# Two transformer blocks in one kernel: openings by tiles, conditioning sums one feed-forward step later

## The chip, the core and the metric

The kernel is one program on one core of a Trainium2 chip. A core has five engines that work side by side and meet only at semaphores: TensorE (PE in the profile; its weight loads are PEld), VectorE (DVE), ScalarE (ACT), GpSimd (POOL) and SyncE (SP), which here only issues transfers. Each engine takes its own instructions strictly in the order in which they are written. SBUF is the memory on the core, PSUM the one that TensorE writes its sums to. The metric is the device time of one execution in microseconds (us), as the median of several.

## What is computed

The reference runs a first block of two layers and then a second block of two layers over 256 tokens of width 1024, in float32.

A layer of the first block is conditioned by a vector `c`: `mod = silu(c) @ ada_w + ada_b`, nine vectors of 1024. It has three sublayers: a SwiGLU feed-forward, a token mixer and another SwiGLU feed-forward (inner width 2816), each as

```
u = h * (1 + scale) + shift
y = (silu(u @ w_gate) * (u @ w_up)) @ w_down        # feed-forward
h = layer_norm(alpha * h + 0.5 * gate * y, g, b)
```

The mixer projects `u` to three branches (a gated convolution, a state-space scan, an attention with compressed keys) and merges them. A layer of the second block is an RMS norm, a projection to attention and mLSTM, an output product, and a feed-forward `relu(u @ w_ff1)**2 @ w_ff2` with inner width 4096.

## The kernel before

Activations are kept transposed: 8 tiles of 128 features by 256 tokens. Weights come from memory as chunks of 128 x 1024 numbers (512 KB) into a ring of nine slots (`stream_weights`, issued by SyncE). A large product is made from three fast ones (`product3`, lines 446 to 453): every float32 operand is split into a high part and a low part (the rest), and the sum high x high + high weight x low activation + low weight x high activation stands for the full product. In the trace line 451 is the first of these, 452 the one with the low activation, 453 the one with the low weight; the tile names `ac_parts`, `h_parts`, `cmp_parts` hold high activations, `u_parts` low ones, `high` the high and `ring_parts` the low weights.

So every chunk needs two preparations before TensorE can take it. ScalarE copies its high part (`high`, line 1054, one of three buffers, so it waits until the chunk three places earlier has been used), then the low part is a subtraction: VectorE makes it for the chunks of the gate and up products (`low`, line 1433), GpSimd for those of the down products (`low_down`, line 1968). Count `lo_g` tells TensorE how many of GpSimd's are ready.

A feed-forward of the first block has 22 slices of the inner width. `step` j of its loop (three passes over six steps, j = 0 to 5; in the trace a step's products are 48 matmuls for the two up chunks of slice f = 1 + j and 24 for the down chunk of the slice before) goes like this.
- TensorE: `up` of the next slice (16 tiles of three products), then `down` of the one before. In step 5 it also multiplies the conditioning sum's 8 tiles with a vector of ones, `column_sums` (line 491), between the two.
- ScalarE: silu of the gate half (line 1084), three high parts with the high part of the hidden slice between them.
- VectorE: `hidden` (line 1501, silu x up), a low part, `hidden_low` (line 1505), in steps 0 to 3 two `add_modulation` each (lines 1379 and 1381: conditioning weights of 128 x 1024 times one number for each partition, added into `eb`), then another low part. In step 5 it fetches the column sums.
- GpSimd: `low_down` for the chunk of the next `down`, then, in steps 0 to 3, two `load_later`: each waits until VectorE has counted the matching addition (`ada.used`) and issues the transfer of the next pass's tile into the same place (line 1944). GpSimd's order is `low_down`, load, load, `low_down`, load, load, and so on; in the third pass of a layer's second feed-forward there are no loads.

A stage opens after a normalization. `enter` on VectorE writes eight tiles of `u`; ScalarE copies each one's high part (count `uhi`), VectorE subtracts to the low part (line 1455, or 2617 in the second block, count `ulo`). `up_first` and its like wait for `ulo` of tile k, then run the three products of that tile for both chunks of the pair. The last feed-forward of the second block opens with one chunk only. There are ten openings: four feed-forwards and two mixers in the first block, two projections and two feed-forwards in the second. While TensorE waits for the norm it multiplies zeros (`products_of_zeros`, 128 x 512, bf16).

In the middle of the mixer two small products (line 727, 60 columns wide) wait for two blocks that GpSimd gathers (line 2015, count `kpe`). There are 16 of these matmuls for block `b = 0` and 16 for `b = 1`, each two records in the trace.

## Time and profile before

| | |
|---|---|
| median of 3 runs | 2673.26 us (2667.3 to 2674.91) |
| the profiled execution | 2667.08 us, span 2665.4 us, mean granted clock of TensorE 0.989 |
| TensorE | 2571.5 us busy, 96% of the span |
| VectorE, ScalarE, GpSimd | 1797.8, 1208.2 and 998.0 us |
| the chain that ended last | 86% of it TensorE, 6% VectorE, 3% GpSimd, 3% ScalarE |

The busy time of an engine is the sum of its instructions; the time that matters is that of the chain, in which each piece is what the next one waited for. The granted clock is the one that the chip gave TensorE: 1.00 is 2.4 GHz, 0.50 is 1.2 GHz. Starts in the rows are counted from the start of the span. In the order of time the stages are: start and first conditioning sums to 43 us; first layer's feed-forward to 247, mixer to 740, second feed-forward to 947; the same for the second layer to 1856; and the second block's two layers from there.

### The profile page before, as it was taken

The page shows a single profiled execution, that of the slowest core. Times are in us where ns is not written, and L with a number is a line of the kernel's source. Part 1 is how long each engine was busy: PE and PEld are TensorE (multiplying, and loading weights), DVE is VectorE, ACT ScalarE, POOL GpSimd, SP SyncE. Part 2 cuts the span into 40 slices and gives each one's busy share as a digit, 9 for nine tenths or more (in the row PEclk, how much of TensorE's full clock was granted, in tenths as well). Part 3 has the DMA queues.
Part 4 walks back from the last instruction along what each step waited for, and adds up shares of the span by engine and source line. Part 5 has one row for each costly group of instructions (what it writes and reads, how often), then busy time and mean ns, then how long its engine had stood idle before and what let it go on. Part 6 is the DMA issues. An engine that isn't in the chain of part 4 may idle for free.

```text
span 2665.4 us, 51124 instructions
## 1 busy us (share of the span) xinstructions
PE 2571.5 (96%) x19552; PEld 2420.5 (91%) x19552; DVE 1797.8 (67%) x2822; ACT 1208.2 (45%) x2019; POOL 998.0 (37%) x588
## 2 busy tenths in 40 slices
PE   3999999999999999999999999999999999999999
PEld 3999999888889989989998878999888999988999
DVE  6775898467686577559984666765853576753676
ACT  2444456245554454444552554444552344652444
POOL 2433986200033233358870000333650244650244
PEclk9999999799999999999999999999999999999999
DMA  8775774233477567767643335775434566433464
GB/s 329 250 271 174 264 228 149 88 102 96 142 252 261 174 229 271 248 216 234 198 130 92 103 96 179 274 243 166 132 115 124 152 186 188 147 122 123 152 188 134
DMA packets 131491, 481.28 MB, mean 181 GB/s; under 512 B 14848, under 2 KB 14848, under 8 KB 130560
## 3 DMA queue, kind: packets, MB, share of 16 engines
q1 hardware_dynamic: 107280, 389.12, 46.1%
q0 software_dynamic: 23040, 83.90, 8.6%
q10 hardware_dynamic: 1008, 6.00, 0.6%
q8 instruction: 113, 1.85, 0.3%
q14 instruction: 50, 0.41, 0.0%
HBM read 475.82 MB, written 3.15 MB: 180 GB/s over the span
## 4 chain that ended last, share of the span: by engine, by line
PE 86%; DVE 6%; POOL 3%; ACT 3%; issue 1%; DVEq 1%; DMA 0%; SPq 0%; ACTq 0%; POOLq 0%
PE ps L451 22%; PE ps L453 21%; PE ps L452 21%; PE ps L693 4%; PE ps L2324 2%; PE ps L543 2%; PE ps L2291 2%; POOL ring_parts L1963 1%; POOL eb L2015 1%; PE ps L491 1%; PE ps L920 1%; DVE ring_parts L1433 1%; DVE eb L1381 1%; PE ps L903 1%; PE ps L793 1%
## 5 line engine op out<-in xcount | busy, mean ns | idle before, releaser
L452 PE MATMUL ps<-u_parts,high 128*128 128x256 f32 x3840 | 1087.9, 283 | 0.0
L452 PEld LDWEIGHTS ps<-u_parts,high 128*128 128x128 f32 x3840 | 737.7, 192 | 0.4
L1054 ACT ACTIVATE high<-ring 128x1024 fp32r<-128x1024 f32 x461 | 485.7, 1056 | 395.2 <-PE ps L453 367.7
L451 PE MATMUL ps<-ac_parts,high 128*128 128x256 f32 x1920 | 550.4, 287 | 18.5 <-DVE u_parts L1455 10.0
L453 PE MATMUL ps<-ac_parts,ring_parts 128*128 128x256 f32 x1920 | 545.5, 284 | 0.0
L1968 POOL TENSOR_TENSOR ring_parts<-ring,high 128x1024 fp32r<-128x1024 f32 x88 | 224.9, 2555 | 473.8 <-ACT high L1054 473.8
L451 PE MATMUL ps<-h_parts,high 128*128 128x256 f32 x1360 | 393.7, 289 | 4.5 <-POOL ring_parts L1963 3.6
L451 PEld LDWEIGHTS ps<-ac_parts,high 128*128 128x128 f32 x1920 | 365.9, 191 | 25.1 <-issue 15.9
L453 PE MATMUL ps<-h_parts,ring_parts 128*128 128x256 f32 x1360 | 386.0, 284 | 0.0
L1963 POOL TENSOR_TENSOR ring_parts<-ring,high 128x1024 fp32r<-128x1024 f32 x138 | 331.3, 2407 | 105.0 <-ACT high L1054 103.7
L453 PEld LDWEIGHTS ps<-ac_parts,ring_parts 128*128 128x128 f32 x1920 | 364.2, 190 | 0.0
L1433 DVE TENSOR_TENSOR ring_parts<-ring,high 128x1024 fp32r<-128x1024 f32 x176 | 217.8, 1239 | 199.0 <-ACT high L1054 188.2
L451 PE MATMUL ps<-pt_parts,high 128*128 128x256 f32 x1216 | 340.8, 280 | 0.8 <-DVE pt_parts L1505 0.8
L452 PE MATMUL ps<-pt_parts,high 128*128 128x256 f32 x1216 | 339.0, 279 | 0.0
L453 PE MATMUL ps<-pt_parts,ring_parts 128*128 128x256 f32 x1216 | 339.0, 279 | 0.0
L2810 POOL TENSOR_TENSOR ring_parts<-ring,high 128x1024 fp32r<-128x1024 f32 x64 | 153.7, 2401 | 366.7 <-ACT high L2384 366.5
L2384 ACT ACTIVATE high<-ring 128x1024 fp32r<-128x1024 f32 x195 | 206.1, 1057 | 178.4 <-PE ps L453 113.8
L451 PEld LDWEIGHTS ps<-h_parts,high 128*128 128x128 f32 x1360 | 262.2, 193 | 13.4 <-issue 5.1
L453 PEld LDWEIGHTS ps<-h_parts,ring_parts 128*128 128x128 f32 x1360 | 262.3, 193 | 0.0
L1944 POOL DMA_DIRECT2D xc<-ada_dram x64 | 34.9, 547 | 554.4 <-DVE u L1446 526.8
L453 PEld LDWEIGHTS ps<-pt_parts,ring_parts 128*128 128x128 f32 x1216 | 230.5, 190 | 0.0
L451 PEld LDWEIGHTS ps<-pt_parts,high 128*128 128x128 f32 x1216 | 228.6, 188 | 1.4 <-DVE pt_parts L1505 1.4
(448 smaller groups left out, 4820.5 us busy)
## 6 DMA issues: line engine op xcount, KB each, us to landing
ring<-stream_dram SPq DMA_DIRECT2D x736, 512.0 KB, 3.7
xc<-ada_dram POOLq DMA_DIRECT2D x84, 512.0 KB, 5.8
z<-ada_dram POOLq DMA_DIRECT2D x36, 512.0 KB, 6.7
qr<-ada_dram POOLq DMA_DIRECT2D x36, 512.0 KB, 6.5
h_aside<-ac ACTq DMA_DIRECT2D x2, 1024.0 KB, 4.4
eb<-ada_dram POOLq DMA_DIRECT2D x4, 512.0 KB, 5.2
h<-h_aside ACTq DMA_DIRECT2D x2, 1024.0 KB, 6.0
conb<-con_dram ACTq DMA_DIRECT2D x1, 1032.0 KB, 7.7
```

The source lines that it names most:

```text
L451: mm(out, hi, xh, start=start, stop=False, **kw)
L452: mm(out, hi, xl, start=False, stop=False, **kw)
L453: return mm(out, lo, xh, start=False, stop=stop, **kw)
L543: last = mm(ps[:, bank, 0:S], ones, src[:, n], start=n == 0, stop=n == ND - 1)
L693: last = mm(out, chunk_tile(m, i, k), src[:, k], start=k == 0, stop=k == 7)
L1054: act(high_of(m, i), chunk_of(m, i), ACT.Copy).then_inc(made, 1)
L1433: tt(low_of(m, i), chunk_of(m, i), high_of(m, i), ALU.subtract).then_inc(sem["lo"], 1)
L1963: nc.gpsimd.tensor_tensor(low_of(m, i), chunk_of(m, i), high_of(m, i), ALU.subtract)\
L1968: nc.gpsimd.tensor_tensor(low_of(m, i), chunk_of(m, i), high_of(m, i), ALU.subtract)\
L2291: last = mm(ps[:, unit(k4), c * S:(c + 1) * S], chunk_tile(m, i, 4 * c + k), (m.att, m.hm)[b][:, k], start=k == 0, stop=k == 3)
L2384: act(high_of(m, i), chunk_of(m, i), ACT.Copy).then_inc(sem["hi"], 1)
L2810: nc.gpsimd.tensor_tensor(low_of(m, i), chunk_of(m, i), high_of(m, i), ALU.subtract)\
```

## The change

Five edits:
1. `pair_by_tiles` replaces the loops of all ten openings. It waits for the high part of tile k (`uhi`), runs the two products that need only that (high x high and low weight x high activation) for both chunks, waits for `ulo` of tile k, and then runs the product with the low activation for both chunks. The chunk counts `done` are raised by the last products, one behind the other.
2. The second block's feed-forward opens with a pair of chunks too, and `down` of slice 0 stands right behind it; the rest keeps its order.
3. `column_sums` in step 5 stands behind `down`.
4. VectorE's conditioning additions stand in steps 1 to 4 in place of 0 to 3. GpSimd's program is not edited.
5. More products of zeros: 14 for 11 and 10 for 8 in the second block's norms, and 8 new ones ahead of the first small product of `kpe`.

```diff
--- before.py
+++ after.py
@@ -453,6 +453,20 @@
     return mm(out, lo, xh, start=False, stop=stop, **kw)
 
 
+def pair_by_tiles(t, mm, m, outs, chunks, xh, xl, high, low):
+
+    for k in range(ND):
+        a, b = k * P, (k + 1) * P
+        high(k)
+        for out, i in zip(outs, chunks):
+            mm(out, high_of(m, i)[:, a:b], xh[:, k], start=k == 0, stop=False, skip_group_check=True)
+            mm(out, low_of(m, i)[:, a:b], xh[:, k], start=False, stop=False, skip_group_check=True)
+        low(k)
+        ends = [mm(out, high_of(m, i)[:, a:b], xl[:, k], start=False, stop=k == ND - 1, skip_group_check=True)
+                for out, i in zip(outs, chunks)]
+    return ends
+
+
 def two(ps, bank, a=0, n=256):
     return ps[:, bank, a:a + 2 * n].rearrange("p (n t) -> p n t", n=2)
 
@@ -569,13 +583,11 @@
             def up_first(i):
 
                 t.wait_ge(sem["lo"], at("lo", 2 * NF * q + 2))
-                for k in range(ND):
-                    t.wait_ge(sem["ulo"], at("ulo", 28 * q + k + 1))
-                    for c in range(2):
-                        last = product3(mm, ps[:, 4 + 2 * c, c * S:(c + 1) * S], m, i + c, k, m.uhi_ffn[:, k], m.ulo[:, k],
-                                        start=k == 0, stop=k == ND - 1, skip_group_check=True)
-                        if k == ND - 1:
-                            last.then_inc(done, 1)
+                ends = pair_by_tiles(t, mm, m, [ps[:, 4 + 2 * c, c * S:(c + 1) * S] for c in range(2)], (i, i + 1),
+                                     m.uhi_ffn, m.ulo, lambda k: t.wait_ge(sem["uhi"], at("uhi", 28 * q + k + 1)),
+                                     lambda k: t.wait_ge(sem["ulo"], at("ulo", 28 * q + k + 1)))
+                ends[0].then_inc(done, 1)
+                ends[1].then_inc(done, 1)
 
             def down(i, f, fk, last=False):
                 t.wait_ge(sem["lo_g"], at("lo_g", q * (NF + FRONT) + fk + 1))
@@ -591,9 +603,9 @@
             with t.Fori(0, 3) as it:
                 for j in range(6):
                     up(cb + 2 + 3 * j, 1 + j, 6 * it + 1 + j)
+                    down(cb + 4 + 3 * j, j, 6 * it + j)
                     if j == 5:
                         column_sums(t, mm, m, ada, ada.summed_group(l, q, it))
-                    down(cb + 4 + 3 * j, j, 6 * it + j)
             for f in range(19, NF):
                 up(cb + 3 * f - 1, f, f)
                 down(cb + 3 * f + 1, f - 1, f - 1)
@@ -615,13 +627,11 @@
                 t.wait_ge(sem["sg"], at("sg", 1))
             if n == 0:
                 low_made(C_GLU + 1)
-                for k in range(ND):
-                    t.wait_ge(sem["ulo"], at("ulo", 8 + k + 1))
-                    for c in range(2):
-                        last = product3(mm, ps[:, unit(3 * c), c * S:(c + 1) * S], m, C_GLU + c, k, m.uhi[:, k], m.ulo[:, k],
-                                        start=k == 0, stop=k == ND - 1, skip_group_check=True)
-                        if k == ND - 1:
-                            last.then_inc(done, 1)
+                ends = pair_by_tiles(t, mm, m, [ps[:, unit(3 * c), c * S:(c + 1) * S] for c in range(2)], (C_GLU, C_GLU + 1),
+                                     m.uhi, m.ulo, lambda k: t.wait_ge(sem["uhi"], at("uhi", 8 + k + 1)),
+                                     lambda k: t.wait_ge(sem["ulo"], at("ulo", 8 + k + 1)))
+                ends[0].then_inc(done, 1)
+                ends[1].then_inc(done, 1)
             else:
                 project(C_GLU + 2 * n, ps[:, unit(j), 0:S]).then_inc(done, 1)
                 project(C_GLU + 2 * n + 1, ps[:, unit(j), S:2 * S]).then_inc(done, 1)
@@ -719,6 +729,9 @@
 
         t.wait_ge(sem["rope"], at("rope", 9))
         for b in range(2):
+            if b == 0:
+                for _ in range(8):
+                    mm(ps[:, unit(j), :], m.zero[:, 0:P], m.zero[:], start=True, stop=True)
             t.wait_ge(sem["kpe"], at("kpe", b + 1))
             for c in range(2):
                 i = C_CK + 2 * b + c
@@ -1516,9 +1529,9 @@
                     hidden(f, fk)
                     low(i + 3, HIGHS * q + 3 * fk + 4)
                     hidden_low(f, fk)
-                    if j < 4:
-                        add_modulation(nc, v, m, ada, ada.group(l, 2 * q, it), ada.summed_group(l, q, it), 2 * j)
-                        add_modulation(nc, v, m, ada, ada.group(l, 2 * q, it), ada.summed_group(l, q, it), 2 * j + 1)
+                    if 1 <= j < 5:
+                        add_modulation(nc, v, m, ada, ada.group(l, 2 * q, it), ada.summed_group(l, q, it), 2 * j - 2)
+                        add_modulation(nc, v, m, ada, ada.group(l, 2 * q, it), ada.summed_group(l, q, it), 2 * j - 1)
                     low(i + 5, HIGHS * q + 3 * fk + 6)
                     if j == 5:
                         keep_columns(nc, v, m, ada, ada.summed_group(l, q, it))
@@ -2072,7 +2085,7 @@
                 t.wait_ge(sem["usq"], at("usq", 8 * k + n + 1))
                 last = mm(ps[:, 0, 0:S], con("mean"), m.sq[:, n], start=n == 0, stop=n == ND - 1)
             last.then_inc(sem["uvar"], 1)
-            products_of_zeros(mm, m, (11, 8)[k])
+            products_of_zeros(mm, m, (14, 10)[k])
 
         rms(0)
         j = 0
@@ -2083,13 +2096,11 @@
             return j + 1
 
         t.wait_ge(sem["lo_g"], at("lo_g", E_Q + 2))
-        for k in range(ND):
-            t.wait_ge(sem["ulo"], at("ulo", k + 1))
-            for c in range(2):
-                last = product3(mm, ps[:, unit(3 * c), c * S:(c + 1) * S], m, E_Q + c, k, m.uhi2[:, k], m.ulo[:, k],
-                                start=k == 0, stop=k == ND - 1, skip_group_check=True)
-                if k == ND - 1:
-                    last.then_inc(done, 1)
+        ends = pair_by_tiles(t, mm, m, [ps[:, unit(3 * c), c * S:(c + 1) * S] for c in range(2)], (E_Q, E_Q + 1),
+                             m.uhi2, m.ulo, lambda k: t.wait_ge(sem["uhi"], at("uhi", k + 1)),
+                             lambda k: t.wait_ge(sem["ulo"], at("ulo", k + 1)))
+        ends[0].then_inc(done, 1)
+        ends[1].then_inc(done, 1)
         j += 1
         project(E_IF, ps[:, unit(j), 0:S]).then_inc(done, 1)
         j += 1
@@ -2349,17 +2360,18 @@
                     x.then_inc(pairs, 1)
             x.then_inc(done, 1)
 
-        t.wait_ge(sem["lo"], at("lo", 1))
-        for k in range(ND):
-            t.wait_ge(sem["ulo"], at("ulo", 8 + k + 1))
-            last = product3(mm, ps[:, 4, 0:S], m, E_FFN, k, m.uhi_ffn[:, k], m.ulo[:, k],
-                            start=k == 0, stop=k == ND - 1)
-        last.then_inc(done, 1)
+        t.wait_ge(sem["lo"], at("lo", 2))
+        ends = pair_by_tiles(t, mm, m, [ps[:, 4 + c, 0:S] for c in range(2)], (E_FFN, E_FFN + 1), m.uhi_ffn, m.ulo,
+                             lambda k: t.wait_ge(sem["uhi"], at("uhi", 8 + k + 1)),
+                             lambda k: t.wait_ge(sem["ulo"], at("ulo", 8 + k + 1)))
+        ends[0].then_inc(done, 1)
+        ends[1].then_inc(done, 1)
+        down(E_FFN + 2, 0, 0)
         with t.Fori(0, 3) as it:
             for q in range(9):
-                up(E_FFN + 1 + 2 * q, 1 + q, 9 * it + 1 + q)
-                down(E_FFN + 2 + 2 * q, q, 9 * it + q)
-        for f in range(28, NF2):
+                up(E_FFN + 3 + 2 * q, 2 + q, 9 * it + 2 + q)
+                down(E_FFN + 4 + 2 * q, 1 + q, 9 * it + 1 + q)
+        for f in range(29, NF2):
             up(E_FFN + 2 * f - 1, f, f)
             down(E_FFN + 2 * f, f - 1, f - 1)
         down(E_FFN + 63, 31, 31, last=True)
```

VectorE at the start of the feed-forward loop before (L1501 is `hidden`, L1433 a low part of weights, L1505 `hidden_low`, L1379 and L1381 the additions; rows without a tile are waits and register instructions):

```order
L1432 REGISTER_ALU
L1433 TENSOR_TENSOR ring_parts<-ring,high 128x1024
L1499 REGISTER_ALU
L1501 TENSOR_TENSOR pt<-ps,pt 128x256
L1432 ISA
L1433 TENSOR_TENSOR ring_parts<-ring,high 128x1024
L1505 TENSOR_TENSOR pt_parts<-pt,pt_parts 128x256
L1381 SCALAR_TENSOR_TENSOR eb<-xc,cvec,eb 128x1024 x2
L1432 REGISTER_ALU
L1433 TENSOR_TENSOR ring_parts<-ring,high 128x1024
```

and from the end of `hidden_low` of step 0 in the changed kernel (13 lines further down: L1514 for L1501, L1446 for L1433, L1518 for L1505, L1392 and L1394 for the additions):

```order
L1518 TENSOR_TENSOR pt_parts<-pt,pt_parts 128x256
L1445 REGISTER_ALU
L1446 TENSOR_TENSOR ring_parts<-ring,high 128x1024
L1512 REGISTER_ALU
L1514 TENSOR_TENSOR pt<-ps,pt 128x256
L1445 ISA
L1446 TENSOR_TENSOR ring_parts<-ring,high 128x1024
L1518 TENSOR_TENSOR pt_parts<-pt,pt_parts 128x256
L1387 ISA
L1391 REGISTER_ALU
L1392 TENSOR_SCALAR eb<-xc,cvec 128x1024
L1394 SCALAR_TENSOR_TENSOR eb<-xc,cvec,eb 128x1024
```

The first two additions stood behind the first `hidden_low`; now a low part, a `hidden`, another low part and the second `hidden_low` are between.

GpSimd in the same loop of the changed kernel (L1981 is `low_down`, L1957 the wait for `ada.used` and the transfer into the conditioning tile):

```order
L1981 TENSOR_TENSOR ring_parts<-ring,high 128x1024
L1961 ISA
L1957 ISA
L1957 DMA xc<-ada_dram 128x1024
L1961 REGISTER_ALU
L1957 ISA
L1957 DMA xc<-ada_dram 128x1024
L1980 ISA
L1981 TENSOR_TENSOR ring_parts<-ring,high 128x1024
```

Nothing moved here: the second `low_down` still stands behind the two loads.

TensorE at the opening of the first feed-forward before:

```order
L451 MATMUL ps<-ac_parts,high 128x256
L452 MATMUL ps<-u_parts,high 128x256
L453 MATMUL ps<-ac_parts,ring_parts 128x256
L451 MATMUL ps<-ac_parts,high 128x256
L452 MATMUL ps<-u_parts,high 128x256
L453 MATMUL ps<-ac_parts,ring_parts 128x256
```

and after (L462, L463 and L465 are the three products in `pair_by_tiles`):

```order
L462 MATMUL ps<-ac_parts,high 128x256
L463 MATMUL ps<-ac_parts,ring_parts 128x256
L462 MATMUL ps<-ac_parts,high 128x256
L463 MATMUL ps<-ac_parts,ring_parts 128x256
L465 MATMUL ps<-u_parts,high 128x256 x2
```

Each tile's six products are the same; the two with `u_parts` are now last, behind a wait of their own.

## Rows read from the trace of the kernel before

**Rows 1.** part 1 of the page: busy time, share of the span, instructions
```profile
PE 2571.5 (96%) x19552; PEld 2420.5 (91%) x19552; DVE 1797.8 (67%) x2822; ACT 1208.2 (45%) x2019; POOL 998.0 (37%) x588
```

**Rows 2.** waits of TensorE: line waited for, us in total, times, longest
```profile
PE ps L451 <- DVE u_parts L1455: 10.0, 4, 5.6
PE ps L451 <- DVE u_parts L2617: 6.1, 4, 1.9
...
PE ps L451 <- DVE ring_parts L1433: 5.2, 4, 1.5
PE ps L727 <- POOL eb L2015: 4.3, 2, 2.2
```

**Rows 3.** timeline of TensorE, one step: start, us, instruction
```profile
881.94 0.29 PE L451 MATMUL ps<-pt_parts,high 128*128 128x256 f32 x1
...
890.49 0.29 PE L451 MATMUL ps<-pt_parts,high 128*128 128x256 f32 x1
```

**Rows 4.** timeline of VectorE, two steps of the same loop
```profile
876.44 0.75 DVE L1379 TENSOR_SCALAR eb<-xc,cvec 128x1024 f32<-128x1024 f32 x1
877.28 1.28 DVE L1381 SCALAR_TENSOR_TENSOR eb<-xc,cvec,eb 128x1024 f32<-128x1024 f32 x1
...
882.56 0.42 DVE L1501 TENSOR_TENSOR pt<-ps,pt 128x256 f32<-128x256 f32 x1 [0.65 <-ACT pt L1084]
883.51 1.23 DVE L1433 TENSOR_TENSOR ring_parts<-ring,high 128x1024 fp32r<-128x1024 f32 x1 [0.52 <-ACT high L1054]
884.65 0.42 DVE L1505 TENSOR_TENSOR pt_parts<-pt,pt_parts 128x256 fp32r<-128x256 f32 x1
884.99 4.63 DVE L1381 SCALAR_TENSOR_TENSOR eb<-xc,cvec,eb 128x1024 f32<-128x1024 f32 x2
```

**Rows 5.** timeline of ScalarE, same step
```profile
887.81 1.06 ACT L1054 ACTIVATE high<-ring 128x1024 fp32r<-128x1024 f32 x1 [1.78 <-PE ps L453]
```

**Rows 6.** timeline of GpSimd: a low part, two issues, a low part
```profile
886.11 2.42 POOL L1968 TENSOR_TENSOR ring_parts<-ring,high 128x1024 fp32r<-128x1024 f32 x1 [5.29 <-ACT high L1054]
...
134.79 0.53 POOL L1944 DMA_DIRECT2D xc<-ada_dram  x1 [1.22 <-DVE eb L1381]
...
268.79 1.09 POOL L1944 DMA_DIRECT2D xc<-ada_dram  x2
269.90 2.40 POOL L1963 TENSOR_TENSOR ring_parts<-ring,high 128x1024 fp32r<-128x1024 f32 x1
```

**Rows 7.** timeline of VectorE in the step of the 134.79 issue
```profile
129.51 4.62 DVE L1381 SCALAR_TENSOR_TENSOR eb<-xc,cvec,eb 128x1024 f32<-128x1024 f32 x2
```

**Rows 8.** timelines of VectorE, ScalarE, TensorE, first layer's second feed-forward opening
```profile
757.41 0.49 DVE L1455 SCALAR_TENSOR_TENSOR u_parts<-u,entry,ac_parts 128x256 fp32r<-128x256 f32 x1 [0.18 <-ACT ac_parts L1065]
757.81 1.22 DVE L1433 TENSOR_TENSOR ring_parts<-ring,high 128x1024 fp32r<-128x1024 f32 x1
...
758.71 1.06 ACT L1054 ACTIVATE high<-ring 128x1024 fp32r<-128x1024 f32 x1 [1.34 <-PE ps L453]
...
759.08 0.39 PE L451 MATMUL ps<-ac_parts,high 128*128 128x256 f32 x1
```

**Rows 9.** timelines of VectorE and TensorE, second block's last opening
```profile
2483.99 0.98 DVE L2617 TENSOR_TENSOR u_parts<-u,ac_parts 128x256 fp32r<-128x256 f32 x2
...
2487.57 0.42 DVE L2776 TENSOR_TENSOR pt_parts<-pt,pt_parts 128x256 fp32r<-128x256 f32 x1 [0.83 <-ACT pt_parts L2564]
...
2485.58 0.28 PE L453 MATMUL ps<-ac_parts,ring_parts 128*128 128x256 f32 x1
...
2488.58 0.28 PE L451 MATMUL ps<-pt_parts,high 128*128 128x256 f32 x1
```

**Rows 10.** windows: busy us of each engine, granted clock (PEclk), DMA
```profile
475.10:478.80 3.70, 3.67 (x33) 3.54 (x31) 3.48 (x7) 2.91 (x7) 3.70 (x8) 1.00 0.47 167
481.80:492.00 10.20, 10.20 (x49) 10.20 (x49) 7.09 (x10) 0.67 (x5) 3.91 (x2) 0.50 0.33 116
1393.30:1403.30 10.00, 9.94 (x46) 9.94 (x47) 7.95 (x11) 0.67 (x5) 4.86 (x3) 0.50 0.46 139
```

## The prediction

> **What bounds the kernel now.** I read the page first: TensorE is busy 2571.5 us of 2665.4 [rows 1], so at most 94 us can be won by filling its gaps, and every other engine has slack on average. Then the waits of TensorE: of those that this change could touch, 10.0 + 6.1 us are waits for low activations at openings, 5.2 us for a low weight part by VectorE, 4.3 us for GpSimd's gathered blocks [rows 2]. The rest of the gaps is mostly the start. Last the timelines of one loop step on each engine. They show that the loop is TensorE's alone: a `down` starts at 881.94, the next at 890.49, 8.55 us later, with no bracketed idle time at either [rows 3]. Call the start of `down` T; all times below are counted from it.
>
> **The additions one step later: what is queued behind them.** On VectorE the move costs nothing by itself. Steps 1 to 4 get what steps 0 to 3 had. And it wins nothing: the low parts that TensorE waits for (5.2 us in 4 waits, one at each feed-forward [rows 2]) are made ahead of step 0's additions, so they come as late as before.
>
> But the additions release GpSimd. Its order is unchanged: `low_down`, load, load, `low_down`. The two loads behind the `low_down` of step j wait for two additions that now run in step j + 1, and the `low_down` of step j + 1, which TensorE needs for its next `down`, is queued behind them. Before, it started at T + 4.17 (886.11) and ended at T + 6.59, 1.96 us ahead of the `down` at T + 8.55 [rows 3, 6]. Now, in a step without backlog:
> - the additions start at T + 3.05 (884.99) [rows 3, 4]. Undisturbed, one takes 1.28 us and the first of a pass 0.75, with 0.09 between (876.44 + 0.75 to 877.28) [rows 4].
> - the issue follows the end of its addition by 0.66 us (129.51 + 4.62 = 134.13, issue at 134.79) and takes 0.53 [rows 6, 7]. A low part follows an issue at once (268.79 + 1.09, then 269.90), and takes 2.40 [rows 6].
> - step 1: 3.05 + 0.75 + 0.09 + 1.28 = 5.17; + 0.66 + 0.53 = 6.36; + 2.40 = 8.76 or 8.8. TensorE wants it at 8.55: it waits 0.25 to 0.3.
>
> In steps 2 to 4 the delay feeds on itself. VectorE's last low part of a step becomes possible at T + 6.93, when ScalarE's high part ends (887.81 + 1.06) [rows 5]. GpSimd's subtraction has started by then, and the two don't run together: in the step shown GpSimd works from 886.11 to 888.53, and the second addition, which could start at 886.36, ends at 889.62, 1.1 us after it [rows 4, 6]. So VectorE's low part comes after GpSimd's, and the next `hidden` after that. What then goes round is a closed loop over two engines, one after the other: `hidden` and `hidden_low` 0.34 each, low part 1.14 (starts 883.51, 884.65, 884.99 [rows 4]), additions 2 x 1.37, hand-over 0.66, issue 0.53, GpSimd's low part 2.40, last low part 1.14. That is 9.29 us, against TensorE's 8.55. TensorE waits 0.7 us in each of the three steps. A pass costs 0.3 + 3 x 0.72 = 2.45 us. Passes with loads are 3 in a first and 2 in a second feed-forward, in two layers: 10. The term is +24.5 us.
>
> Bounds: if the hand-over were hidden (0.66 less per round), the loop would take 8.63 and the term nearly vanish, 0 to 3 us; the other end is the first rival's, +40. The value of 24.5 is from rows of the same instructions, so I take it.
>
> **The column sums behind the sixth `down`**: 8 small matmuls change places with 72 others of the same length in sum. They wait for the additions of step 4, which end before T + 7 of that step, while they start some 11 us after its T. VectorE's fetch of them comes behind a low part that is later still. 0, with 0 to 1 us a pass if VectorE had to wait for them; I take 0.
>
> **Openings.** VectorE sets the pace, not TensorE: the last low activation ends at 757.90, and TensorE is then just a tile behind it [rows 8]. Starting early on high parts is therefore given back tile by tile; what remains is the last tile, of which 2 products and not 6 come behind the last low part. That is four pitches of 0.12 us (72 products in 8.55 us [rows 3]), 0.48 us for TensorE. But the next thing it waits for is ScalarE's and VectorE's: here the low part of 757.81 + 1.22 = 759.03, after which it starts at 759.08 whatever it did before [rows 8]. The chain behind that starts with ScalarE's high part at 758.71, released by the first chunk's last product, which comes two pitches earlier: 0.24 us. Eight openings (feed-forwards, mixers, projections) give 8 x 0.24 = 1.9 us; from 0 to 8 x 0.48 = 3.8.
>
> The second block's feed-forward gains more. There the last low activation ends at 2484.97, two more products close both chunks at about 2485.3, and silu, square and the low hidden part follow. Before, they ended at 2487.99, behind a first chunk whose last product started at 2485.58, and `down` started at 2488.58, after the whole second chunk [rows 9]. Now that product starts 0.5 us earlier, `down` can start at about 2487.5, so 1.0 us is won, and TensorE stands for about 2.2 us instead of working on the second chunk. Two of them: -2.0 us, and from -4 to +2 if the new gap or the denser opening moves the clock.
>
> **Zeros and the clock.** The extra zeros in the norms are 3 and 2 of about 0.22 us: they fit into waits of up to 1.9 us [rows 2]. The 8 ahead of the small `kpe` products are about 1.7 us and push the first block's products towards the second block's wait, which is 2.1 to 2.2 us long [rows 2]: they fill it and end before GpSimd does, so no time is lost. What they may win is clock. Through 3.7 us of the same small products without a gap the granted clock stayed at 1.00 (2.4 GHz); after the wait it was 0.50 (1.2 GHz) for 10.2 us in the first layer and 10.0 in the second, with TensorE busy throughout [rows 10]. If it stays up, half of that is won, 5.1 us a layer. The trace doesn't tell whether 0.4 us of idle time in place of 2.1 is enough, among products this narrow. Bounds 0 and 10.2; I take one of two layers, -5.
>
> **Sum.** Against the profiled execution: +24.5 - 1.9 - 2.0 - 5 = +15.6, so 2667.1 + 15.6 = 2682.7 us. That execution was at the low end of the three runs, 6.2 us under the median; I add that: 2689 us.
>
> **Rivals.**
> 1. *The lock falls the other way (slower still).* At T + 6.9 GpSimd's subtraction starts and VectorE's last low part becomes possible at T + 6.93: nearly a tie in the first steps. If VectorE is first, GpSimd's ends 1.14 us later, near T + 10.5, and TensorE waits 2.0 us; the step behind catches up. Two such steps a pass are 4 us, 40 in all: 2667.1 + 40 - 9 + 6.2 = 2704 us. For it: the closeness. Against it: step 1 is no tie (6.36), and from then on VectorE is the later one.
> The Trainium skill, "SBUF - State Buffer", section "Who interferes with whom", says that whichever engine issues first gets the shared port pair for the whole instruction and the other blocks fully. The trace agrees with the blocking, 1.1 us as told above; by that rule the order of start is all that parts this rival from my forecast.
> 2. *No wait arises (faster).* GpSimd's slack of 1.96 us absorbs the move, because hand-over and issue cost less when GpSimd already stands at the wait. It decides when the round gets under 8.55, that is 0.74 us shorter. Then only the gains are left: 2667.1 - 9 + 6.2 = 2664 us, and 2659 with the clock kept in both layers. Against it: 0.66 was measured with GpSimd standing idle at just such a wait (1.22 us before the issue [rows 6]).
> 3. *The wait arises, the clock gain doesn't.* Zeros leave the clock as it was, the new gap of 2.2 us costs what the pair wins: 2667.1 + 24.5 + 6.2 = 2698 us.
> 4. *The change does not do what it says:* if `ada.used` were counted apart from the additions the loads would not be late; the code counts it on the additions themselves. Part of rival 2.
>
> **How the numbers follow.** The forecast has 0.60, with a range of its own of 2679 to 2698; rival 1 0.16, rival 2 0.11, rival 3 0.13. Under 0.3%, 8 us on 2673.3, a measurement of this kernel can't tell a change from none. Faster, under 2665: most of rival 2, 0.09. Within: the rest of it and the low end of the forecast (both layers keep the clock), 0.02 + 0.11 = 0.13. Slower: 0.78. The range reaches down to near rival 2 and up to rival 1: 2667 to 2708.
>
> **What would show it.** GpSimd's `low_down` of steps 1 to 4 starting at T + 6.4 to 7.5, right behind an issue; a new wait of TensorE for it, some 30 to 40 times, 25 us in all; rounds of 9.3 us for three steps. In place of 16.1 us of waits for low activations, less, and about 2 us for the low hidden part at the second block's feed-forwards. The clock after `kpe`, per layer. I am wrong if TensorE's waits for `low_down` stay under 5 us in all, or if the time is under 2665.

## The result

| | before | after |
|---|---|---|
| median | 2667.29 us (2663.17 to 2674.91, 13 runs) | 2687.53 us (2675.66 to 2691.05, 13 runs) |
| ratio after to before, 95% interval | | 1.0063 (1.0052 to 1.0074) |
| the profiled execution | 2667.08 us, span 2665.4 | 2690.51 us, span 2688.8 |
| mean granted clock | 0.989 | 0.987 |

The changed kernel is slower by 0.63%, which is 16.8 us of the median before, with an interval from 13.9 to 19.7. (The two medians alone are 20.2 us apart; this text goes by the ratio.) Forecast were 2689 us, slower, by a sum of +15.6. The loss is the wait that was predicted. Two gains that were forecast, of the pair and of the zeros, were not there, and one gain, a faster pace of TensorE, was not foreseen.

### The profile page after: what moved, and what is told of

It is laid out like the page before. It is cut to its first block, busy times and chain, and to the rows that moved or that the text cites. A ratio compares the mean times of both kernels' runs of the same rounds, so it can differ in the third digit from the quotient of the medians.

```text
span 2688.8 us, 51176 instructions
## 1 busy us (share of the span) xinstructions
PE 2587.0 (96%) x19578; PEld 2425.1 (90%) x19578; DVE 1801.2 (67%) x2822; ACT 1211.3 (45%) x2019; POOL 988.6 (37%) x588
## 4 chain that ended last, share of the span: by engine, by line
PE 77%; DVE 8%; POOL 5%; issue 4%; ACT 4%; DVEq 1%; DMA 0%; POOLq 0%; SPq 0%; ACTq 0%
PE ps L451 18%; PE ps L453 18%; PE ps L452 18%; PE ps L703 4%; DVE eb L1394 2%; PE ps L2335 2%; PE ps L557 2%; POOL ring_parts L1981 2%; PE ps L2302 2%; DVE ring_parts L1446 2%; POOL ring_parts L1976 1%; ACT high L1067 1%; POOL eb L2028 1%; PE ps L505 1%; PE ps L933 1%
## 5 line engine op out<-in xcount | busy, mean ns | idle before, releaser
L452 PE MATMUL ps<-u_parts,high 128*128 128x256 f32 x3680 | 1039.9, 283 | 0.0
L452 PEld LDWEIGHTS ps<-u_parts,high 128*128 128x128 f32 x3680 | 704.5, 191 | 0.4
L451 PE MATMUL ps<-ac_parts,high 128*128 128x256 f32 x1824 | 519.3, 285 | 6.5 <-DVE ring_parts L1446 6.5
L453 PE MATMUL ps<-ac_parts,ring_parts 128*128 128x256 f32 x1824 | 516.8, 283 | 0.0
L1446 DVE TENSOR_TENSOR ring_parts<-ring,high 128x1024 fp32r<-128x1024 f32 x176 | 293.0, 1666 | 222.0 <-ACT high L1067 216.8
L451 PE MATMUL ps<-h_parts,high 128*128 128x256 f32 x1328 | 383.9, 289 | 5.0 <-POOL ring_parts L1976 4.3
L453 PE MATMUL ps<-h_parts,ring_parts 128*128 128x256 f32 x1328 | 377.1, 284 | 0.0
L1976 POOL TENSOR_TENSOR ring_parts<-ring,high 128x1024 fp32r<-128x1024 f32 x138 | 331.4, 2408 | 104.5 <-ACT high L1067 103.2
L451 PE MATMUL ps<-pt_parts,high 128*128 128x256 f32 x1216 | 343.0, 282 | 16.4 <-POOL ring_parts L1981 11.2
L451 PEld LDWEIGHTS ps<-ac_parts,high 128*128 128x128 f32 x1824 | 345.9, 190 | 7.7 <-DVE ring_parts L1446 7.7
L453 PEld LDWEIGHTS ps<-ac_parts,ring_parts 128*128 128x128 f32 x1824 | 343.8, 188 | 0.0
L1981 POOL TENSOR_TENSOR ring_parts<-ring,high 128x1024 fp32r<-128x1024 f32 x88 | 214.0, 2431 | 309.4 <-ACT high L1067 308.8
L2822 POOL TENSOR_TENSOR ring_parts<-ring,high 128x1024 fp32r<-128x1024 f32 x64 | 153.9, 2405 | 370.5 <-ACT high L2396 370.3
L1957 POOL DMA_DIRECT2D xc<-ada_dram x64 | 34.9, 546 | 662.8 <-DVE u L1459 533.4
```

Of the source, the lines that this page charges most:

```text
L451: mm(out, hi, xh, start=start, stop=False, **kw)
L452: mm(out, hi, xl, start=False, stop=False, **kw)
L453: return mm(out, lo, xh, start=False, stop=stop, **kw)
L1446: tt(low_of(m, i), chunk_of(m, i), high_of(m, i), ALU.subtract).then_inc(sem["lo"], 1)
L1976: nc.gpsimd.tensor_tensor(low_of(m, i), chunk_of(m, i), high_of(m, i), ALU.subtract)\
L1981: nc.gpsimd.tensor_tensor(low_of(m, i), chunk_of(m, i), high_of(m, i), ALU.subtract)\
```

## The profile after

Part 1 of the page of the changed kernel, the answer to [rows 1]:

```profile
PE 2587.0 (96%) x19578; PEld 2425.1 (90%) x19578; DVE 1801.2 (67%) x2822; ACT 1211.3 (45%) x2019; POOL 988.6 (37%) x588
```

The 26 instructions more on TensorE are the zeros. The waits of TensorE in the changed kernel, the answer to [rows 2] (line waited for, us in total, times, longest; line numbers are those of the changed kernel, L1981 is `low_down`):

```profile
PE ps L451 <- POOL ring_parts L1981: 11.2, 39, 0.3
PE ps L462 <- ACT ac_parts L1078: 7.9, 4, 5.1
PE ps L451 <- DVE ring_parts L1446: 6.5, 6, 1.5
...
PE ps L451 <- DVE pt_parts L2788: 4.3, 2, 2.2
...
PE ps L740 <- POOL eb L2028: 0.9, 2, 0.5
```

The first row shown is new: 39 waits for GpSimd's low part, four in each of the ten passes with loads but the first, which has three. The openings now wait for high parts (7.9 for 10.0 us), the second block's feed-forwards wait for the low hidden part, 2.2 us each, and the wait between the two `kpe` blocks has shrunk from 2.2 to 0.5 us.

How a loop step looks is seen on three engines. TensorE in steps 4 and 5 of the second pass of the first layer's second feed-forward (start, us, instruction, idle time before it and what ended it), the answer to [rows 3], and two `down` of the third pass, which has no loads:

```profile
861.93 0.38 PE L451 MATMUL ps<-pt_parts,high 128*128 128x256 f32 x1 [0.32 <-POOL ring_parts L1981]
...
871.00 0.38 PE L451 MATMUL ps<-pt_parts,high 128*128 128x256 f32 x1 [0.30 <-POOL ring_parts L1981]
...
889.85 0.28 PE L451 MATMUL ps<-pt_parts,high 128*128 128x256 f32 x1
...
898.33 0.28 PE L451 MATMUL ps<-pt_parts,high 128*128 128x256 f32 x1
```

With loads a step takes 9.07 us, without them 8.48. The bracket tells only 0.30 of the 0.59 lost. The rest is in how such rows are made: idle time is counted from the modelled end of the matmul before, 0.28 after its start, while a product follows the one before it by 0.12 (so 0.16 is left out), and the first product after a wait holds up the second by 0.22 instead of 0.12. A wait of 0.3 us in these rows is a loss of nearly 0.6. Their sum of 11.2 us therefore shows only about half of the loss.

GpSimd in the same step, the answer to [rows 6]:

```profile
866.55 0.57 POOL L1957 DMA_DIRECT2D qr<-ada_dram  x1 [4.75 <-DVE eb L1394]
867.93 0.53 POOL L1957 DMA_DIRECT2D qr<-ada_dram  x1 [0.81 <-DVE eb L1394]
868.47 2.40 POOL L1981 TENSOR_TENSOR ring_parts<-ring,high 128x1024 fp32r<-128x1024 f32 x1
```

and ScalarE's high part that this low part is made from:

```profile
864.98 1.06 ACT L1067 ACTIVATE high<-ring 128x1024 fp32r<-128x1024 f32 x1 [1.30 <-PE ps L453]
```

GpSimd stands 4.75 us at the wait for the first addition and 0.81 at that for the second. The high part had ended at 866.04, 2.4 us earlier, and the low part comes only behind the second issue. It starts 6.54 us after the `down` at 861.93; forecast was T + 6.4 to 7.5. VectorE in the same step, the answer to [rows 4]:

```profile
864.62 2.65 DVE L1394 SCALAR_TENSOR_TENSOR eb<-qr,cvec,eb 128x1024 f32<-128x1024 f32 x2
868.95 3.01 DVE L1446 TENSOR_TENSOR ring_parts<-ring,high 128x1024 fp32r<-128x1024 f32 x1 [1.69 <-ACT high L1067]
871.88 0.41 DVE L1514 TENSOR_TENSOR pt<-ps,pt 128x256 f32<-128x256 f32 x1
872.22 1.21 DVE L1446 TENSOR_TENSOR ring_parts<-ring,high 128x1024 fp32r<-128x1024 f32 x1
873.35 0.41 DVE L1518 TENSOR_TENSOR pt_parts<-pt,pt_parts 128x256 fp32r<-128x256 f32 x1
```

The two additions end at 867.27 (864.62 + 2.65), 0.66 us before the issue at 867.93. The low part of 868.95 has 3.01 us in place of 1.21: it started 0.48 us after GpSimd's and could go on only when that ended at 870.87. So GpSimd was first, and so it is in every other step with loads of this trace, by 0.38 to 0.91 us. The Trainium skill, "SBUF - State Buffer", section "Who interferes with whom", says that a VectorE instruction with two inputs in SBUF contends with a GpSimd instruction that reads SBUF; these two rows agree, with 1.8 us lost to it.

The closed loop of the prediction can be read off, from the end of one GpSimd low part to the end of the next: 1.01 to `hidden` (870.87 to 871.88), 0.34 to the next low part, 1.13 to `hidden_low`, 0.34 to the additions, 2.65 for these, 0.66 to the second issue, 0.54 for it and 2.40 for the low part. The sum is 9.07 us, and that is TensorE's step.

Openings, TensorE of the changed kernel: the second feed-forward of the first layer ([rows 8]) and the last one ([rows 9]):

```profile
756.67 0.36 PE L462 MATMUL ps<-ac_parts,high 128*128 128x256 f32 x1 [0.95 <-ACT ac_parts L1078]
...
763.65 0.38 PE L451 MATMUL ps<-ac_parts,high 128*128 128x256 f32 x1 [0.58 <-DVE ring_parts L1446]
...
2509.72 0.36 PE L451 MATMUL ps<-pt_parts,high 128*128 128x256 f32 x1 [2.16 <-DVE pt_parts L2788]
```

The early start is given back: at 763.65 TensorE waits for a weight's low part, 0.58 us. At 2509.72 stands the forecast wait of 2.2 us for the low hidden part.

Stage by stage, in us, between the same landmarks in both traces (where TensorE starts a run of zeros in a norm, and the first `down` of a feed-forward):

| stage | before | after | difference |
|---|---|---|---|
| start to the first `down` | 63.60 | 62.99 | -0.6 |
| first feed-forward: layer 1 from its first `down`; layer 2 | 191.38; 209.00 | 196.55; 213.88 | +5.2; +4.9 |
| mixer, layer 1 | 493.41 | 493.42 | 0.0 |
| mixer, layer 2 | 488.24 | 494.84 | +6.6 |
| opening of the second feed-forward, layer 1 | 16.84 | 16.60 | -0.24 |
| second feed-forward: the rest of layer 1; layer 2 | 193.19; 209.03 | 196.11; 211.58 | +2.9; +2.55 |
| second block, layer 1 | 399.36 | 398.5 | -0.9 |
| second block, layer 2 | 394.18 | 397.15 | +3.0 |

They add up to the difference of the spans, 23.4. The feed-forwards of the first block, +15.3 in all, are the change. The +6.6 is half-clock time in the second mixer (17.1 us of it before, 30.7 after), which the runs below show to come and go. Of the +3.0 in the last row 2.0 are a slower pace of TensorE, 30 steps of 5.67 us for 5.60, which comes and goes as well (see the last section).

## The experiments

All were timed beside the kernel before (its medians there: 2668.31, 2669.93 and 2669.26 us). Ratios are to before, with the 95% interval.

**1 and 2. Is it the loads behind the additions?** `adds_back` is the changed kernel with the additions in steps 0 to 3 again:

```diff
-                    if 1 <= j < 5:
-                        add_modulation(..., 2 * j - 2)
-                        add_modulation(..., 2 * j - 1)
+                    if j < 4:
+                        add_modulation(..., 2 * j)
+                        add_modulation(..., 2 * j + 1)
```

> The changed kernel with VectorE's additions back in steps 0 to 3; openings, column sums, pair and zeros as changed. Theory (the loads in GpSimd's queue hold up the low parts): TensorE's 39 waits for GpSimd's low parts in the loops go, a pass with loads takes the 52.6 us of one without, ten passes give 23 us: about 2664 us, slightly under the kernel before. Rival (the time is lost in the mixer's clock and the new openings): it stays within 4 us of 2687.

`loads_follow` leaves VectorE as changed, and moves GpSimd's two loads one step later too:

```diff
-                    if j < 4 and more:
-                        for k in range(2 * j, 2 * j + 2):
+                    if 1 <= j < 5 and more:
+                        for k in range(2 * j - 2, 2 * j):
```

> The changed kernel with GpSimd's loads moved along, from steps 0 to 3 to steps 1 to 4, so that each load stands behind the low part of the step in which its addition runs; VectorE as changed. Theory: what cost time is the order within GpSimd, not the place of the additions, so this gives the same 2664 us as the additions put back. Rival: additions in steps 1 to 4 cost something on VectorE by themselves: then it stays above the additions put back, by up to 20 us.

Measured: `adds_back` 2666.6 us, 0.9982 (0.9968 to 0.9997); `loads_follow` 2666.97 us, 0.9985 (0.9969 to 1.0002). In neither trace is there a row of TensorE waiting for L1981. GpSimd of `loads_follow`:

```profile
850.68 2.41 POOL L1981 TENSOR_TENSOR ring_parts<-ring,high 128x1024 fp32r<-128x1024 f32 x1 [3.87 <-ACT high L1067]
853.03 0.57 POOL L1957 DMA_DIRECT2D z<-ada_dram  x1
854.82 0.54 POOL L1957 DMA_DIRECT2D z<-ada_dram  x1 [1.22 <-DVE eb L1394]
859.22 2.41 POOL L1981 TENSOR_TENSOR ring_parts<-ring,high 128x1024 fp32r<-128x1024 f32 x1 [3.86 <-ACT high L1067]
```

The low part now waits for its own input, ScalarE's high part, and the loads come behind it, with the additions as late as in the changed kernel. So it is not the place of the additions that costs, but that GpSimd's loads did not move with them: 1.0063 / 0.9985 = 1.0078, 20.8 us.

**3. The additions alone.** `only_adds` is the kernel before with edits 3 and 4 only.

```diff
+                    down(cb + 4 + 3 * j, j, 6 * it + j)
                     if j == 5:
                         column_sums(...)
-                    down(cb + 4 + 3 * j, j, 6 * it + j)
...
-                    if j < 4:
+                    if 1 <= j < 5:
```

> The kernel before with only the additions in steps 1 to 4 and the column sums behind the sixth down product. Theory: ten passes at 2.3 us: 2667.3 + 23 = 2690 us, 40 waits of TensorE for GpSimd's low part of about 0.3 us shown each, rounds of 9.1 us. Rival (the openings or the pair cost the time): 2667 us.

Measured: 2682.0 us, 1.0042 (1.0027 to 1.0058), and in its waits of TensorE the same row as in the changed kernel:

```profile
PE ps L451 <- POOL ring_parts L1968: 11.4, 39, 0.3
```

The wait is there in full, but the time is 8 us under what was expected. The trace shows one reason: its steps without waits take 8.48 us and not 8.55, worth 5.4 us (more on that below). The rest stays open: by the two traces the four loops take 16.7 us more, by the ratio the kernel 11.2 (7.2 to 15.5).

**4 and 5. The zeros ahead of `kpe`.** `no_kpe_zeros` is the changed kernel without them, `kpe_zeros_only` the kernel before with them alone.

```diff
-            if b == 0:
-                for _ in range(8):
-                    mm(ps[:, unit(j), :], m.zero[:, 0:P], m.zero[:], start=True, stop=True)
```

> The changed kernel without the 8 products of zeros ahead of the first small product. If they did nothing for the clock: 2687 +- 2 us. If they spoiled it (the profile after shows 30.7 us at half clock in the second layer's mixer, before 17.1): about 2681. If they helped on average, as forecast with -5: about 2692.

> The kernel before with only the 8 products of zeros ahead of the first small product. Theory (formed after the first four runs: the zeros take away the pause between the two runs of narrow products and leave TensorE at half clock longer in the mixer): about 2667 + 6 = 2673 us, mixers with some 50 us at half clock in sum, before 44. Rival 1 (my forecast's): -5 us, 2662. Rival 2 (the 6 us between the changed kernel and the one without these zeros were the chance of the day): 2667 +- 2.

Measured: `no_kpe_zeros` 2681.15 us, 1.0046 (1.0028 to 1.0064, six runs), which overlaps with the changed kernel's 1.0063 (1.0052 to 1.0074); `kpe_zeros_only` 2668.36 us, 0.9999 (0.9982 to 1.0017). TensorE of `kpe_zeros_only` and its clock over the 70 us around (busy us and instructions of PE, PEld, DVE, ACT, POOL, then the granted clock):

```profile
475.79 1.89 PE L724 MATMUL ps<-zero 128*128 128x512 bf16 x8
477.52 3.68 PE L730 MATMUL ps<-eb,ring 128*128 128x60 f32 x32
481.64 6.09 PE L730 MATMUL ps<-eb,ring 128*128 128x60 f32 x32 [0.45 <-POOL eb L2018]
```

```profile
470.00:540.00 70.00, 69.55 (x432) 61.79 (x431) 34.87 (x71) 18.15 (x36) 16.44 (x25) 0.85 0.33 99
```

The wait is filled as forecast (0.45 us is left), and yet the second 32 products take 6.09 us where the first take 3.68: the clock falls all the same. The zeros save nothing that can be measured. The harm of 6 us that the first of the two runs had suggested isn't there either.

**6. Everything but the zeros and the late loads.** `follow_no_zeros` is `loads_follow` without the `kpe` zeros:

```diff
-            if b == 0:
-                for _ in range(8):
...
+                    if 1 <= j < 5 and more:
+                        for k in range(2 * j - 2, 2 * j):
```

> The changed kernel with GpSimd's loads moved along and without the 8 products of zeros. If both causes add: 2667.0 - 6.3 = about 2661 us, the fastest of all. If the zeros matter only beside the held-up loads: 2667.

Measured: 2669.43 us, 0.9994 (0.9983 to 1.0006). The 2661 us for the case that the zeros do harm are missed; they don't. Nor is there any gain of openings and pair that this timing could show.

**7, 8 and 9. The zeros in the wait itself.** In `zeros_between` (`loads_follow` otherwise) the eight zeros stand ahead of `b == 1`, between the two runs of small products. They overwrite the first product's result in its bank, so that kernel leaves the first block of compressed keys out; it has the same instructions as `loads_follow`, eight of them in another place.

```diff
-            if b == 0:
+            if b == 1:
                 for _ in range(8):
```

> The same kernel with the 8 products of zeros, but ahead of the second small product, where TensorE stands 2.1 us for GpSimd. If it is wide products in the pause that keep the clock up: some us under the kernel without zeros, at best 2656. If the clock falls because of the long run of narrow products before and after, whatever stands in the pause: the same as without zeros, 2661 +- 2. If any zeros here harm: 2667.

Measured: 2660.86 us, 0.9965 (0.9949 to 0.998). `follow_zeros_in_wait` does it without touching the result, with 11 zeros of 384 columns in the free part of the bank, and `zeros_in_wait_only` is the kernel before with these zeros alone:

```diff
+            if b == 1:
+                for _ in range(11):
+                    mm(ps[:, unit(j), P:4 * P], m.zero[:, 0:P], m.zero[:, P:4 * P], start=True, stop=True)
             t.wait_ge(sem["kpe"], at("kpe", b + 1))
```

> The changed kernel with the loads moved along and the zeros ahead of the second small product, written to columns of the bank that hold nothing (11 of 384 columns). As the kernel with zeros_between, which overwrote the first product: 0.9965 of the kernel before, about 2660 us, the fastest. If that kernel's gain was chance or came from the overwritten values: 0.9985 to 0.9994.

> The kernel before with only these zeros, 11 of 384 columns ahead of the second small product. If wide products in the pause keep the clock up: 3 to 7 us less than the kernel before, with less than 44 us at half clock in the two mixers. If not: no change.

Measured: 2659.39 us, 0.9962 (0.9949 to 0.9975), and 2661.12 us, 0.997 (0.9956 to 0.9984). TensorE of `zeros_in_wait_only`, and the same window of it:

```profile
474.75 3.68 PE L730 MATMUL ps<-eb,ring 128*128 128x60 f32 x32
478.26 1.95 PE L724 MATMUL ps<-zero 128*128 128x384 bf16 x11
480.58 3.78 PE L730 MATMUL ps<-eb,ring 128*128 128x60 f32 x32 [0.37 <-POOL eb L2018]
```

```profile
470.00:540.00 70.00, 69.63 (x467) 60.92 (x465) 37.45 (x82) 19.27 (x38) 15.39 (x23) 0.93 0.36 107
```

The same 1.9 us of zeros and a rest of the wait of the same size (0.37), but now the second run of products takes 3.78 and not 6.09 us. One window is one execution; over all profiles, with 470 to 540 us for the first mixer and 1385 to 1475 for the second, and half-clock time worked out as 2 x (1 - clock) x length:

| zeros | kernels | mean clock, mixer 1 and 2 | half-clock us, both |
|---|---|---|---|
| none | 6 (before, `only_adds`, `no_kpe_zeros`, `follow_no_zeros`, `openings_only`, `pair_only`) | 0.848, 0.895 | 40 |
| ahead of the first run | 5 (after, `adds_back`, `loads_follow`, `kpe_zeros_only`, `one_load_later`) | 0.822, 0.884 | 46 |
| between the runs | 3 | 0.897, 0.937 | 26 |

At half the clock TensorE's products of 256 columns follow each other by 0.213 us and otherwise by 0.119 (rows in the last section), so 0.44 of the 14 us between the first row and the last is time saved, 6 us. The timed runs say 8.0 us (0.3% of 2669; 4 to 12 by the interval) for `zeros_in_wait_only`. The order of the first two rows is not borne out by time: 0.9999 for `kpe_zeros_only`. Within a row single profiles differ by more: the second window has 0.83 in the changed kernel and 0.94 in `kpe_zeros_only`. Such a difference is the +6.6 us in the second mixer (13.6 us more at half clock, 0.44 of it is 6.0); no run here ties it to the change.

**10. The openings.** `openings_only` is the kernel before with `pair_by_tiles` in the eight openings that had a pair:

```diff
-                for k in range(ND):
-                    t.wait_ge(sem["ulo"], at("ulo", 28 * q + k + 1))
...
+                ends = pair_by_tiles(...)
```

> The kernel before with pair_by_tiles in the eight openings that had a pair already; the second block's feed-forward, the zeros and the additions as before. Theory: 8 x 0.24 = 1.9 us less, 2665.4 us; the waits at the openings get shorter by about 0.5 us each, and most of it comes back as waits for low parts of weights. Rival (TensorE's early start is kept): 8 x 0.48 + the 0.5 us of earlier start, 5 us or more.

Measured: 2669.82 us, 0.9998 (0.9988 to 1.0009). Its waits of TensorE:

```profile
PE ps L462 <- ACT ac_parts L1075: 7.9, 4, 5.1
PE ps L451 <- DVE ring_parts L1443: 6.7, 6, 1.5
...
PE ps L462 <- ACT cmp_parts L2416: 2.5, 2, 1.4
```

10.0 us of waits for low activations have become 7.9 for high ones, and 5.2 in 4 for a low weight part 6.7 in 6: the wait has moved, and what is left over is too small for this measurement. Its trace shows it: from the norm's zeros to the first `down` the last three feed-forwards of the first block take 16.60, 16.58 and 16.59 us, before 16.84, 16.83 and 16.85.

**11. The pair in the second block's feed-forward.** `pair_only` is the kernel before with edit 2 alone:

```diff
-        t.wait_ge(sem["lo"], at("lo", 1))
...
+        ends = pair_by_tiles(t, mm, m, [ps[:, 4 + c, 0:S] for c in range(2)], (E_FFN, E_FFN + 1), ...)
+        down(E_FFN + 2, 0, 0)
         with t.Fori(0, 3) as it:
             for q in range(9):
-                up(E_FFN + 1 + 2 * q, 1 + q, 9 * it + 1 + q)
+                up(E_FFN + 3 + 2 * q, 2 + q, 9 * it + 2 + q)
```

> The kernel before with only the second block's feed-forward opened by a pair, down of slice 0 behind it. Theory: -2.0 us, 2666 us, and TensorE stands 2.2 us twice for the low hidden part. Rival (the stand costs clock): +1 to +2.

Measured: 2668.88 us, 1.0005 (0.9989 to 1.0021), with the wait of the changed kernel in it:

```profile
PE ps L451 <- DVE pt_parts L2791: 4.3, 2, 2.2
```

**12. How much delay does GpSimd's low part bear?** `one_load_later` is the changed kernel with one of the two loads of each step moved on, so that the low part waits for one late addition and not two:

```diff
-                    if j < 4 and more:
-                        for k in range(2 * j, 2 * j + 2):
+                    if j < 5 and more:
+                        for k in range(max(2 * j - 1, 0), min(2 * j + 1, ND)):
```

> The changed kernel with only the second load of each pair moved behind the next low part in GpSimd's queue, so that a low part stands behind one addition of its own step and not two. If the arithmetic of the queue is right: addition ends at T + 4.33, hand-over 0.66, issue 0.53, low part 2.40 = T + 7.92, 0.6 us before TensorE wants it; the waits for GpSimd's low parts in the loops go, and the time is that of the loads moved along, 0.9985 of the kernel before, about 2666 us. If any load queued ahead costs (a rival without a threshold): about half of the 20 us stay, 2677.

Measured: 2665.04 us, 0.9979 (0.9964 to 0.9995), without one row of a wait for L1981. Its GpSimd:

```profile
850.58 0.53 POOL L1957 DMA_DIRECT2D qr<-ada_dram  x1 [5.05 <-DVE eb L1394]
851.12 2.43 POOL L1981 TENSOR_TENSOR ring_parts<-ring,high 128x1024 fp32r<-128x1024 f32 x1
853.50 0.57 POOL L1957 DMA_DIRECT2D qr<-ada_dram  x1
```

The low part still comes behind a load that waits, but 1.38 us (one addition) earlier, and steps take 8.48 to 8.65 us. There is a threshold, and the changed kernel's first late step is just over it: in the forecast the low part ends at 8.76 us, against a step of 8.55. The place of one load decides on 22 us (1.0063 / 0.9979).

## Why the prediction was right, point by point

**The wait: right, in place, mechanism and size.** Forecast were 30 to 40 waits and +24.5 us. The trace has 39. A pass with loads takes 8.48 + 8.91 + 9.07 + 9.08 + 9.07 + 10.37 = 54.98 us from `down` to `down`, a pass without them in the same kernel 5 x 8.48 + 10.24 = 52.64. That is 2.34 a pass (forecast 2.45), 23.4 in ten; a little less in fact, since the first passes lose less. Two parts of the round were a little too large: the two additions take 2.65 and not 2.74 us, and `hidden` follows the end of GpSimd's low part by 1.01 us and not 1.14, so it is 9.07 and not 9.29 us. The forecast figure that missed by most is "25 us in all" for the waits as listed: they sum to 11.2, for the reason given with the rows of TensorE.

**Rival 1, the lock falling the other way, did not occur.** GpSimd's low part started 0.48 us ahead of VectorE's in the steps shown; after step 1 it is no tie, as was argued. **Rival 2, no wait,** is what `loads_follow` and `adds_back` show when the loads stand right; the changed kernel isn't it.

**The pace of TensorE was not foreseen: -5.4 us.** In the kernel before, a step without waits takes 8.55 us ([rows 3]), in the changed one 8.48, with the same instructions: 0.45 us a pass, in 12 passes. It is the larger part of why `only_adds` came out at 2682 and not 2690. What the loops lose on balance can be read directly: from the first to the last `down` the four feed-forwards take 177.59, 178.35, 178.38 and 178.38 us before and 182.97, 181.41, 183.69 and 181.39 after, 16.8 us more in all. With the pace added back the wait alone is 22 to 23 us.

**The column sums: 0 forecast, nothing found.** `adds_back` has them moved and no wait, and the same four stretches take 177.85, 178.36, 178.34 and 178.35 us.

**Openings: -1.9 forecast, nothing in the timing** (interval -3 to +2 us). The mechanism is right to the hundredth where it was worked out (16.84 to 16.60), and again in the two feed-forwards of layer 2 (16.83 to 16.61 and 16.85 to 16.60). For the mixers and projections it was not read off, so that it sums to 1.9 is not shown. `only_adds`, `adds_back`, `loads_follow` and `no_kpe_zeros` need 0.22 us less for this stretch, with the new opening and without (16.38 and 16.62); why is open, but the difference of 0.24 holds among them too.

**The pair: -2.0 forecast, not found.** From the start of the norm's zeros to the first `down` it is 11.74 us for 12.49, so 0.75 is won of the 1.0 forecast. But in layer 1 the first step behind it takes 7.25 us for 5.59, in layer 2 5.76. Windows of the changed kernel over these two steps (columns as in [rows 10]):

```profile
2111.30:2118.50 7.20, 7.17 (x48) 7.20 (x49) 5.20 (x4) 2.12 (x3) 2.54 (x1) 0.76 0.51 172
2509.70:2515.50 5.80, 5.78 (x49) 5.80 (x50) 4.79 (x4) 2.01 (x3) 2.55 (x1) 1.00 0.57 206
```

Behind the wait of 2.2 us the granted clock is 0.76 in the one and 1.00 in the other, and the step at 0.76 is 1.7 us longer (0.24 of 7.2). That is the end of the forecast's bounds at which the new gap moves the clock (+2), in one layer of two. The other traces agree: of the nine kernels with the pair, eight have one such step of 7.2 to 7.3 us in one of their two layers, and the five without it have none. So in most executions profiled 1.7 us were lost once and 0.75 won twice, and over both nothing is won that can be measured: 1.0005 (0.9989 to 1.0021).

**The zeros ahead of `kpe`: -5 forecast, 0 measured.** This step failed. The prediction said that the trace couldn't tell, gave 0 to 10.2 as bounds and took one of two layers; what came is the lower bound. It looked only at how much idle time is left. (It also priced half-clock time at one half of its length; the rows in the last section give 0.44.) The trace has 0.42 to 0.45 us left of 2.1 and the clock falls anyway. What counts in these kernels is where the wide products stand: between the two runs of narrow ones, with the same rest of the wait, they are worth 8 us (4 to 12). Why is not shown. The Trainium skill, "TensorE: Matmul & The Clock Gate", section "What's actually happening", says that the throttled state is the default and activity releases it. The trace agrees in the direction (more work in the wait, less half-clock time), but idle time alone does not order these kernels.

**Rival 3, the wait without the gains, is in substance what happened.** The clock gain did not come, and the pair won nothing. Its sum was +24.5 and 2698 us; that the result lies at 2687.5, near the forecast, is mostly due to a pace of TensorE that neither had.

**Sum.** With the terms as the traces show them: +16.8 (loops, the wait less the pace) - 0.7 to -1.9 (openings) + 0 (pair) + 0 (zeros) = 15 to 16 us; forecast +15.6; measured 16.8 (13.9 to 19.7). The main term and its mechanism were right, but that the total is this near is luck: the zeros and the pair were taken 7 us too good, the pace 5.4 and the wait 1 to 2 too bad.

**A version faster than both.** `follow_zeros_in_wait`, that is all edits, with GpSimd's loads moved along with the additions and the zeros put into the wait, runs in 2659.39 us: 0.38% under before and 1% under the changed kernel (0.9962 / 1.0063). `zeros_in_wait_only` shows that nearly all of it is the zeros.

## What to carry to other kernels

When work moves on one engine, look at what waits for it on the others, and at what is queued behind that wait: the two loads did not compute anything, yet a low part on TensorE's path stood behind them, and moving one of them on by a step is worth 22 us. Work out the closed round over all engines and hold it against the step of the engine that bounds; a round that is longer costs its excess in every step, and the idle brackets of the profile showed only half of it here. To keep the clock up through a wait, put wide products of zeros into the wait itself, as here between two runs of narrow ones, and then time it in many runs, since the half-clock time of one profile proves nothing.

## What was not expected of the hardware

- *TensorE has two paces for one stream of the same instructions.* A first-block step takes 8.55 us, in which products of `up` follow each other by 0.1191 us and those of `down` by 0.1180, or 8.48 us, with 0.1200 and 0.1137. A whole trace mostly stays with one: before, `adds_back`, `loads_follow` and `follow_zeros_in_wait` with 8.55, the changed kernel, `only_adds` and `no_kpe_zeros` with 8.48. It isn't the program of TensorE, which is the same in `adds_back` and the changed kernel. In `one_load_later` single feed-forwards go over from 8.55 to 8.48 behind steps of 8.60 and 8.59, and stay there until the stage ends, so a short wait at a `down` seems to set it. That isn't all: `kpe_zeros_only` and `zeros_in_wait_only` each have two steps of 8.48 behind one of 8.8, and are back at 8.55 after the next column sums. The second block has two paces as well, 5.60 and 5.67 us, one layer of the changed kernel in each. The slower one costs 2.0 us a layer and is in 10 of the 28 layers of the 14 traces, in kernels with and without the change. What in the chip does this stays open; it was not tried separately.
- *The clock falls among narrow products after 0.4 us of idle time.* In the changed kernel it is at 1.2 GHz from 487.7 us, behind 32 products of 60 columns, a wait of 0.42 us and some more of them:

```profile
487.70:494.50 6.80, 6.80 (x33) 6.80 (x33) 5.75 (x10) 0.67 (x5) 2.58 (x2) 0.50 0.63 203
```

  Three products of 256 columns take 0.64 us there, in place of 0.36: 1.8 times as long and not twice.

```profile
491.10 0.41 PE L451 MATMUL ps<-h_parts,high 128*128 128x256 f32 x1
491.74 0.41 PE L451 MATMUL ps<-h_parts,high 128*128 128x256 f32 x1
```

- *VectorE's low part behind a GpSimd one took 3.01 us and not 1.21,* and ended 1.1 us after GpSimd's: nearly all of its work was done after the other had ended.
